# Hybrid diffusion trunk on one core: the last two modulation blocks of a layer computed in the router stage

## The reference

```python
mod = (jax.nn.silu(cond) @ lw['w_ada'] + lw['b_ada'])[:, None, :]
sh1, sc1, gt1, sh2, sc2, gt2 = jnp.split(mod, 6, axis=-1)
h = rmsnorm(x, lw['g_norm1']) * (1.0 + sc1) + sh1
# u = h @ w_in: three branches (differential attention, bidirectional gated
# delta rule, neighbourhood attention) and their gates; merged = gated sum
x = x + gt1 * (merged @ lw['w_out'])
h2 = rmsnorm(x, lw['g_norm2']) * (1.0 + sc2) + sh2
x = x + gt2 * expert_choice_ffn(h2, lw['w_router'], lw['w_e_gate'], lw['w_e_up'], lw['w_e_down'])
```

## Time and profile before

| | |
|---|---|
| median of 3 runs | 3517.86 us (3516.3 to 3520.94) |
| profiled execution | 3521.77 us, its span 3520.0 us |
| mean granted TensorE clock | 0.983 of 2.4 GHz |
| busy: PE, DVE, ACT, POOL | 96%, 37%, 20%, 4% of the span |
| delta stage, layer 0 | about 200 to 789 us of the span |
| router stage, layer 0 | about 1085 to 1193 us of the span |
| chain of waits, by engine | PE 87%, DMA 7%, ACT 3%, DVE 2% |

### The profile page before, as it was taken

The page is one execution under the profiler, slowest core; times in us unless marked ns, Lnnn a source line. Parts: engine busy times, 40 slices in busy tenths (PEclk is TensorE's granted clock), DMA queues, the critical chain, the costliest instruction groups (busy, mean ns, idle before and its releaser), DMA issues.

```text
span 3520.0 us, 47854 instructions
## 1 busy us (share of the span) xinstructions
PE 3388.4 (96%) x20939; PEld 1901.7 (54%) x20939; DVE 1300.3 (37%) x2503; ACT 706.7 (20%) x1536; POOL 157.9 (4%) x179
## 2 busy tenths in 40 slices
PE   7999999999999899999989999999999998999998
PEld 4557767765554544444455577677655554443433
DVE  3354443337542321212243644433464522211213
ACT  3131111115332200000021311111254322000001
POOL 1000000000100000000100000000000000000000
PEclk9999999999999899999999999999999999999998
DMA  7242332341241699999941424232512408999997
GB/s 224 97 125 71 89 100 63 102 115 71 77 171 56 248 383 387 387 395 386 383 141 48 133 63 120 69 107 58 173 48 72 168 31 299 379 396 389 391 389 270
DMA packets 218049, 675.69 MB, mean 192 GB/s; under 512 B 9779, under 2 KB 22297, under 8 KB 214257
## 3 DMA queue, kind: packets, MB, share of 16 engines
q1 hardware_dynamic: 198096, 613.97, 49.6%
q0 software_dynamic: 13312, 43.05, 4.7%
q10 hardware_dynamic: 6432, 15.62, 1.2%
HBM read 605.91 MB, written 66.68 MB: 191 GB/s over the span
## 4 chain that ended last, share of the span: by engine, by line
PE 87%; DMA 7%; ACT 3%; DVE 2%; issue 1%; ACTq 0%; POOL 0%; DVEq 0%; POOLq 0%
PE unit L839 12%; PE unit L787 11%; PE unit L1353 10%; PE work L1356 8%; PE work L1353 6%; PE unit L851 4%; PE unit L830 3%; PE unit L1228 3%; PE unit L870 3%; PE unit L781 3%; DMA arena<-in_w_e_gate 2%; DMA ring<-in_w_e_gate 2%; PE unit L1176 2%; PE work L1041 2%; PE work L1075 2%; PE unit L797 1%
## 5 line engine op out<-in xcount | busy, mean ns | idle before, releaser
L839 PE MATMUL unit<-hT,ring 128*128 128x512 f32 x1024 | 475.5, 593 | 0.0
L1353 PE MATMUL unit<-ring,arena 128*64 128x512 f32 x1568 | 357.1, 601 | 5.3 <-DVE arena L2287 5.3
L2300 DVE SCALAR_TENSOR_TENSOR arena<-work,arena 64x512 f32<-64x512 f32 x64 | 47.9, 749 | 669.4 <-PE work L1353 668.3
L1356 PE MATMUL work<-ring,arena 128*32 128x256 f32 x4608 | 275.4, 382 | 3.9 <-DMA ring<-in_w_e_gate 1.9
L839 PEld LDWEIGHTS unit<-hT,ring 128*128 128x128 f32 x1024 | 177.9, 191 | 140.6 <-issue 140.6
L1353 PEld LDWEIGHTS unit<-ring,arena 128*64 128x64 f32 x1568 | 110.8, 138 | 226.6 <-issue 221.0
L1356 PEld LDWEIGHTS work<-ring,arena 128*32 128x32 f32 x4608 | 136.5, 109 | 164.1 <-issue 79.6
L787 PE MATMUL unit<-hT,ring 128*128 128x512 f32 x512 | 221.1, 592 | 0.0
L1833 ACT ACTIVATE arena<-work 128x512 f32<-128x512 f32 x32 | 19.1, 597 | 846.4 <-PE work L1368 846.4
L1353 PE MATMUL work<-ring,arena 128*64 128x512 f32 x736 | 168.2, 599 | 2.5 <-ACT arena L1834 2.1
L787 PE MATMUL unit<-arena,ring 128*128 128x512 f32 x384 | 166.8, 592 | 0.0
(11 more groups left out here) (448 smaller groups left out, 4737.1 us busy)
## 6 DMA issues: line engine op xcount, KB each, us to landing
ring<-in_w_e_gate SPq DMA_DIRECT2D x50, 2048.0 KB, 14.6
ring<-in_w_e_up SPq DMA_DIRECT2D x48, 2048.0 KB, 14.9
ring<-in_w_e_down SPq DMA_DIRECT2D x46, 2048.0 KB, 16.4
ring<-in_w_in SPq DMA_DIRECT2D x32, 2048.0 KB, 15.4
ring<-in_w_ada SPq DMA_DIRECT2D x24, 2048.0 KB, 8.8
arena<-in_w_e_down SPq DMA_DIRECT2D x18, 2048.0 KB, 15.1
arena<-in_w_e_up SPq DMA_DIRECT2D x16, 2048.0 KB, 14.4
arena<-in_w_e_gate SPq DMA_DIRECT2D x14, 2048.0 KB, 17.5
```

Of the source, the lines that this page charges most:

```text
L839: last = mm(bank[:, :], w[:, k, m * P:(m + 1) * P], hT[:, k, 0:TS], start=k == 0, stop=k == KD - 1)
L1353: last = mm(big[SLS * c:SLS * c + SLS, :], x, w[:, kk, 512 * c:512 * c + 512], start=k == 0, stop=k == KD - 1)
L1356: last = mm(low[SLOTP * c:SLOTP * c + SLOTP, 0:256], xp, w[:, kk, 256 * c:256 * c + 256], start=k == 0, stop=k == KD - 1)
```

## The change

Blocks 10 and 11 leave `FILL` and come last in `PLAN`, behind the output projection's chunks. `EARLY_ADA` is the number of blocks that stay early. TensorE issues block 10 behind the transposes of tiles 4 and 5 and block 11 behind the context tokens' logits, and both folds behind the transposes of the slots. The folds use bank W[3], the copied rows lie in the arena. The bias of `gt2` is added in an instruction of its own behind expert 0's modulated rows. The matrices `gates` and `gatep` are spread behind the first half of expert 0's gate product, in the banks that the down product uses, and the down product of each expert waits for `gates_ready`. On ScalarE the two copies and the two folds come behind `keep_h(8, 10)`, and the copies of the gate matrices behind `keep_x`.

```diff
--- before.py
+++ after.py
@@ -64,9 +64,10 @@
 LATE = [("gc", 0), ("gc", 1)]
 BRANCHES = "bca"
 FILL = []
+EARLY_ADA = 10
 _a = 4
 for _s in [("va", 0), ("qa", 0), ("kc", 0), ("ka", 0), ("qc", 0), ("vc", 0)] + [("g" + b, i) for b in "ab" for i in (0, 1)]:
-    if _a < 12:
+    if _a < EARLY_ADA:
         FILL += [("ada", _a), _s, ("fold", _a)]
         _a += 1
     else:
@@ -75,6 +76,7 @@
 PLAN = [("ada", a) for a in range(4)] + [("qb", 0), ("kb", 0), ("vb", 0), ("zb", 0)]
 PLAN += [_f for _f in FILL if _f[0] != "fold"] + LATE
 PLAN += [("br" + b, i) for b in BRANCHES for i in (0, 1)] + [("wo", 0), ("wo", 1)]
+PLAN += [("ada", a) for a in range(EARLY_ADA, 12)]
 
 
 def kind_of(name):
@@ -398,7 +400,8 @@
         sqsum = rt[:, 1, :]
         xflat = xT.rearrange("p k t -> p (k t)")
         stage = [xflat[:, 512 * i:512 * i + 512] for i in range(NSTAGE)]
-        adarow = [at(7680, (512,)), xflat[:, 512 * NSTAGE:512 * NSTAGE + 512]]
+        adarow = 4 * [at(7680, (512,))] + (EARLY_ADA - 4) * [xflat[:, 512 * NSTAGE:512 * NSTAGE + 512]]
+        adarow += [at(2560 + 512 * i, (512,)) for i in range(12 - EARLY_ADA)]
         (gE, gL, gAT, gD, gDT, gI, gD2, gD2T, gD4, gP, gX, c32, gN, gVB, gKB, gKD) = [
             at(17408 + 512 * i, (H, P)) for i in range(16)]
         gXn, gY, gZT, gV0, gV = gD2, gD2T, gD, gD4, gP
@@ -465,6 +468,9 @@
 
         def tile_t(t):
             return slice(t * P, (t + 1) * P)
+
+        def fold_bank(a):
+            return W[5] if a < EARLY_ADA else W[3]
 
         def last_banks(t):
             return ((W[0], W[1]), (W[3], W[4]), (W[2], W[5]))[t % 3]
@@ -585,7 +591,7 @@
                 sp.dma_start(O["new_diff_v"][0, l].rearrange("t h d -> t (h d)"), aV[:, NTS, :])\
                     .then_inc(sig["new_v_stored"], 16)
                 spilled(*SPILLED[-1])
-                sp.wait_ge(sig["mod_ready"], 12 * (l + 1))
+                sp.wait_ge(sig["mod_ready"], 12 * l + EARLY_ADA)
                 back(flat(K[1]), "kc", 0, "k_loaded")
                 sp.wait_ge(sig["delta_turned"], H * (l + 1))
                 back(flat(Q[1]), "qc", 0, "q_loaded")
@@ -805,7 +811,8 @@
                 if l or a:
                     pe.wait_ge(sig["mod_ready"], 12 * l + a)
                 for m in range(4):
-                    last = mm(W[5][:, 2 * m:2 * m + 2], adarow[a >= 4][:, tile_t(m)], C("fold")[:, 0:2], start=True, stop=True)
+                    last = mm(fold_bank(a)[:, 2 * m:2 * m + 2], adarow[a][:, tile_t(m)], C("fold")[:, 0:2],
+                              start=True, stop=True)
                 last.then_inc(sig["ada_folded"], 1)
                 yield
 
@@ -1211,7 +1218,7 @@
                         project(l, "br" + s, half, dict(a=oaT, b=obT, c=ocT)[s], kk=H)
                         if s == BRANCHES[0] and half == 0:
                             sub_sums()
-                pe.wait_ge(sig["mod2_ready"], l + 1)
+                pe.wait_ge(sig["mod2_ready"], 2 * l + 1)
                 for g in range(2):
                     for k in range(KD):
                         mm(W[0][:, 96 + NE * g:96 + NE * g + NE], mod[:, 24 + k, g:g + 1].to_broadcast([P, P]), wrt[:, k, :],
@@ -1277,6 +1284,8 @@
                 for m in range(4):
                     wo_prompt(1, m)
                 turn_x(4, 6, W[4:6], xT)
+                for _ in ada(l, EARLY_ADA):
+                    pass
                 pe.wait_ge(sig["prompt_added"], 2 * l + 2)
                 router_rows(1, W[3], slice(TS, T), 0)
                 router_rows(1, W[3], slice(TS, T), 4).then_inc(sig["logits_rowed"], 1)
@@ -1286,17 +1295,9 @@
                 last.then_inc(sig["tokens_summed"], 1)
                 pe.wait_ge(sig["logits_copied"], 2 * l + 2)
                 fold_logits((NTS,))
+                for _ in ada(l, EARLY_ADA + 1):
+                    pass
                 turn_x(6, 2 * NT, W[4:6], xT)
-                pe.wait_ge(sig["unit_emptied"], wo_unit(l, 1, None) + 1)
-                for c in range(2):
-                    for k in range(4):
-                        mm(ps[0][SLS * c:SLS * c + SLS, tile_t(k)],
-                           mod[:, 40 + 4 * c + k, 0:1].to_broadcast([P, SLS]), ident, start=True, stop=True)
-                for c in range(4):
-                    for k in range(2):
-                        last = mm(ps[1][SLOTP * c:SLOTP * c + SLOTP, tile_t(k)],
-                                  mod[:, 40 + 2 * c + k, 1:2].to_broadcast([P, SLOTP]), ident, start=True, stop=True)
-                last.then_inc(sig["gates_spread"], 1)
                 pe.wait_ge(sig["aff_ready"], 2 * l + 2)
                 tr(W[1][0:NE, 0:TP], aff[:, NTS, :], ident).then_inc(sig["aff_turned"], 1)
 
@@ -1309,9 +1310,25 @@
                     last = mm(W[5][SLOTP * c:SLOTP * c + SLOTP, 0:NE], best[0:NE, SLS:SLS + SLOTP],
                               ident[0:NE, 0:NE], start=True, stop=True)
                 last.then_inc(sig["slot_turned"], 1)
-                pe.wait_ge(sig["gates_ready"], l + 1)
+                for a in range(EARLY_ADA, 12):
+                    for _ in fold(l, a):
+                        pass
                 turn_x(2 * NT, 3 * NT, (W[4], ps[1]), xT)
                 pe.wait_ge(sig["slots_ready"], 3 * l + 2)
+
+                def spread_gates():
+
+                    pe.wait_ge(sig["slots_ready"], 3 * l + 3)
+                    pe.wait_ge(sig["mod2_ready"], 2 * l + 2)
+                    for c in range(2):
+                        for k in range(4):
+                            mm(W[2][SLS * c:SLS * c + SLS, tile_t(k)],
+                               mod[:, 40 + 4 * c + k, 0:1].to_broadcast([P, SLS]), ident, start=True, stop=True)
+                    for c in range(4):
+                        for k in range(2):
+                            last = mm(W[5][SLOTP * c:SLOTP * c + SLOTP, tile_t(k)],
+                                      mod[:, 40 + 2 * c + k, 1:2].to_broadcast([P, SLOTP]), ident, start=True, stop=True)
+                    last.then_inc(sig["gates_spread"], 1)
 
                 def turn_rows(e):
 
@@ -1337,6 +1354,8 @@
                         else:
                             pe.wait_ge(sig["left_copied"], l * NE + e)
                             pe.wait_ge(sig["right_copied"], l * NE + e)
+                    if kind == "d" and half == 0:
+                        pe.wait_ge(sig["gates_ready"], l + 1)
                     if kind == "d" and half == 0:
                         pe.wait_ge(sig["hidT_ready"], l * NE + e + 1)
                     if kind == "g" and half == 0:
@@ -1372,6 +1391,8 @@
                 for e in range(NE + 1):
                     if e < NE:
                         expert_chunk(e, "g0")
+                    if e == 0:
+                        spread_gates()
                     if e == 0:
                         turn_x(3 * NT, 4 * NT, (W[4], ps[1]), xT)
                         pe.wait_ge(sig["x_kept"], 4 * NT * (l + 1))
@@ -1456,11 +1477,11 @@
             def ada(l, a):
                 n = unit_no(l, "ada", a)
                 big = unit(n)
-                emptied(a_(adarow[a >= 4], big[:, :], ACT.Copy))
+                emptied(a_(adarow[a], big[:, :], ACT.Copy))
 
             def fold(l, a):
                 act.wait_ge(sig["ada_folded"], 12 * l + a + 1)
-                a_(mod[:, 4 * a:4 * a + 4, :], W[5][:, 0:8].rearrange("p (m g) -> p m g", g=2), ACT.Copy)\
+                a_(mod[:, 4 * a:4 * a + 4, :], fold_bank(a)[:, 0:8].rearrange("p (m g) -> p m g", g=2), ACT.Copy)\
                     .then_inc(sig["mod_ready"], 1)
 
             def square(n, k, words=T):
@@ -1751,7 +1772,7 @@
                                     a_(rt1[:, h, 0:TS], W[h][:, :], ACT.Sqrt, bias=eps, scale=1.0 / P)
                                 a_(rt1[:, :, TS:T], h4(W[4]), ACT.Sqrt, bias=eps, scale=1.0 / P)\
                                     .then_inc(sig["sub_rooted"], 1)
-                act.wait_ge(sig["mod2_ready"], l + 1)
+                act.wait_ge(sig["mod2_ready"], 2 * l + 1)
 
                 a_(stat[:, 95:96], eps, ACT.Sqrt)
                 for u in range(KD):
@@ -1815,10 +1836,14 @@
                 keep_h(6, 8)
                 weights_exp(1, prompt)
                 keep_h(8, 10)
+                for a in range(EARLY_ADA, 12):
+                    ada(l, a)
+                for a in range(EARLY_ADA, 12):
+                    fold(l, a)
+                keep_x(2 * NT, 4 * NT)
                 act.wait_ge(sig["gates_spread"], l + 1)
-                a_(gates, ps[0][:, :], ACT.Copy)
-                a_(gatep, ps[1][:, 0:256], ACT.Copy).then_inc(sig["gates_ready"], 1)
-                keep_x(2 * NT, 4 * NT)
+                a_(gates, W[2][:, :], ACT.Copy)
+                a_(gatep, W[5][:, 0:256], ACT.Copy).then_inc(sig["gates_ready"], 1)
 
                 def gate_hidden(e):
 
@@ -2077,9 +2102,9 @@
                 for br in range(2):
                     nb = 2 * l + br
                     if br:
```

(11 more changed lines are left out.)

## The result

The changed kernel took 3529.37 us (median of 6 runs, 3526.31 to 3535.69) beside 3518.89 us (6 runs, 3516.3 to 3526.37) for the kernel before in the same measurement: ratio 1.0029, 95% interval 1.0016 to 1.0043, some 10 us slower. I had forecast 3518 us with 3508 to 3527 for the range; the time is outside, on the slow side. The profiled execution took 3526.7 us, span 3524.9.

What follows compares the result with a forecast made beforehand. TensorE, busy 96% of the span, was taken as the bound. Per layer, 4.5 us won in the delta stage met 4.5 us of router-side cost (2.6 + 1.0 + 0.4 + 0.5): no change, 3518 us, range 3508 to 3527.

Steps and rivals of the forecast that it cites:

- Delta stage, -4.5 us a layer: Delta stage without two blocks: attention starts earlier, -4.5 us a layer, bounds -5.5 (nothing exposed) and -3.
- what could be late next: Attention's start: K and Q, down by about 778, and V were checked and held not late; no size given.
- rival (4): Attention's start: the clock falls at TensorE's new waits, up to 1.5 us a layer, 3521 us; chance 0.1.
- Block 10, 0: Router stage, behind the transposes of tiles 4 and 5: hidden in TensorE's wait for GpSimd, 0, bounds 0 and 2 us.
- Block 11, +2.6: Router stage, ahead of the exponential: fully on the path, 1.94 us at full rate, 3.9 at half, taken as 2.6.
- Last store and gather's issue, +1.0: Router stage: last row store lands beside a load in 7.2 us, gather issued 1.0 us later than by the slots alone.
- The gather, +0.4: Gather of expert 0's rows: the longer measured time beside a load, 7.18 us, taken, costing 0.4 us a layer.
- rival (1): Router stage: loads hold the gather, stores 3 us later, gather 10 us; +5.8 us a layer, 3529 us; chance 0.14.
- Folds, 0: Router stage, ahead of transposes: 1.6 us hidden since TensorE waits for the gather, taken as 0, bounds 0 and 1.6.
- Gate matrices, +0.5: Behind expert 0's first half gate product: delay mostly caught up in a load-bound expert stage, 0.5 us, bounds 0 and 2.3.
- rival (2): Router stage hides nearly everything and denser TensorE work keeps the clock up; -4.7 us a layer, 3508 us; chance 0.12.
- a large effect has no source: Whole kernel: 5.5 us of TensorE work per layer is moved and none removed, so no change was expected.

Runs made afterwards that it cites:

- e3: Changed kernel with ScalarE's squares and root of the last group ahead of its copy of the last gap's filler; 3526.95 us, 1.0010 of the kernel before.
- e8: Changed kernel with gate matrices ahead of expert 0, squares before filler copy, two loads held, two transposes ahead of block 11; 3504.30 us, 0.9959 of before.
- e5: Kernel before, with the load of expert 0's fourth half held until the gathered rows have landed; 3515.19 us, 0.9984 of the kernel before.
- e4: Changed kernel with the loads of expert 0's two up halves held until its rows have landed; 3526.68 us, 1.0012 of the kernel before.
- e9: e8 with block 10 folded in TensorE's wait for VectorE's maxima; 3501.28 us, 0.9942 of the kernel before.
- e1: Changed kernel with the gate matrices spread ahead of expert 0's first product; 3524.12 us, 1.0007 of the kernel before.
- e2: Changed kernel with six filler places taken off the delta stage's start, so the list ends as before; 3533.39 us, 1.0029 of the kernel before.
- e7: Changed kernel with only block 11 moved, to block 10's place, and block 10 back in the delta stage; 3527.82 us, 1.0019 of the kernel before.
- e10: e8 without the hold on expert 0's third and fourth half loads; 3514.93 us, 0.9983 of the kernel before.
- e11: e8 with block 11 again ahead of the transposes of steps 6 and 7; 3512.25 us, 0.9977 of the kernel before.
- e12: e8 with ScalarE's copy of the last gap's filler again ahead of the squares; 3512.64 us, 0.9977 of the kernel before.

## Why the prediction was wrong

The terms were the right ones and are separate, as the experiments show: each can be taken away by itself. The sum was wrong because one gain was lost by half and three costs were under-sized. Over both layers the delta stage gave 4.8 us less than forecast, the gather cost 3.3 us more, the gate matrices 4.0 and block 11 1.4; the last store and the issue cost 0.7 less. By the prediction's steps:

- **Delta stage, -4.5 us a layer: measured -2.1 / -2.1.** The head turns do run closer, and attention did not wait for K, Q or V. The step that failed is the question what could be late next: K, Q and V were the whole list. What I left out is that a shift of six places also moves the end of each filler product against ScalarE's fixed order of copies. One now ends in the last tick of the gap ahead of the squares, so its copy, which ScalarE issues first, goes at 772.08, and the squares wait. It was a copy that was late. e3 gives 1.5 us back, and e8, where the clock stays up as well, reaches -5.3 / -5.2: the bound of -5.5 was near the truth for a kernel without that copy.
- **Clock at the new waits.** I named it as a rival (4), for attention's start at 1.5 us a layer, and held it within no change. It fell elsewhere: behind the wait ahead of the first head turn, which the copy had made longer (5.30 us for 3.60, 1.7 us a layer). At attention's start, where I looked for it, it was 1.00 (784 to 800).
- **Block 10, 0: right.** 1.90 us in the wait for GpSimd, 3.58 us to the column sums as before.
- **Block 11, +2.6: measured +3.1 / +3.5.** The clock fell within the block (1.00 from 1168 to 1169, 0.76 in the next microsecond, then 0.50); the mechanism and the order on ScalarE were right.
- **Last store and gather's issue, +1.0: measured +0.6 / +0.7.** The store lands in 6.6 / 6.7 us, where 7.2 was taken.
- **The gather, +0.4: measured +2.5 / +1.6.** This is the second step that failed, on rival (1)'s ground. I took 7.18 us as the price "beside a load". By e5 a gather alone needs 4.1 us, and 6.23 was a gather with a load beside it for 5.4 of its 6.2 us (issued at 1180.15, 8.4 us to landing). In the changed kernel the load issued at 1184.15 lands after 12.5 us, at 1196.6, and is there from the gather's first microsecond to its last. The Trainium skill (DMA: Bandwidth & Descriptors, Queues, rings and completion order) says that a DMA engine takes turns between the queues that have work. An estimate from that rule and e5's figure: with two busy queues throughout, 4.1 us become 8.2. The runs agree roughly: 8.69 and 8.76 were measured, 8.1 to 10.0 in all kernels without the hold that have a moved block. For the kernel before, with the load there for 5.4 us, the same estimate gives 6.8, where 6.2 was measured. The rule that I used against the slower case for the store was the one that gave the gather's price.
- **Folds, 0: right only because the gather was late.** With the loads held they are the bound (e4), and 2.3 / 2.6 us of the stage (e8 to e9).
- **Gate matrices, +0.5: measured +2.6 / +2.4 in expert 0, and not caught up.** This is the third step that failed. I took the expert stage as bound by its weight loads, from one row of 18.02 us on the chain. But TensorE is busy for 495.7 of the 500 us from 1246 to 1746 in the kernel before, and waits for loads for 2.0 us there and 2.8 in layer 1, in the changed kernel for 1.3 and 1.9: that is all there was to give back. The window and the two waits of the kernel before, layer 0 (window as above; waits in us in total, times, longest):

```profile
1246.00:1746.00 500.00, 495.69 (x4438) 200.27 (x4434) 97.77 (x206) 25.28 (x58) 44.69 (x48) 1.00 1.03 388
...
PE work L1356 <- DMA arena<-in_w_e_gate: 1.4, 2, 0.9
PE work L1356 <- DMA ring<-in_w_e_gate: 0.6, 1, 0.6
```

The other experts took 0.3 us more in layer 0; the 2.4 us less in layer 1 are within what that stretch varies by. Of the cost, 2.1 us are the matrices and the rest is expert 0's first product at half clock a little longer (6.54 us for 6.05). That their place can also bring this product to 3.65 us, as in e1, I had not seen: rival (2) had that gain, but from denser work in general.

The sum that I made was 4.5 - 4.5 = 0; that measured in the stages is 9.1 - 2.1 in layer 0 and 5.5 - 2.1 in layer 1. The reasoning that "a large effect has no source", since TensorE's work is only moved, was the wrong guide: the moved work stays the same, and waits and half clock are what it is exchanged for. Rival (1) was right in sign, and in half of its mechanism: the loads slow the gather. But its 3 us of a late store did not come, the gather needed 8.7 us and not 10, and it left the delta stage and the gate matrices as forecast. That its number, 3529 us, is the one measured is luck.

What stays open: which of the two clock levels a wait leads to. With a wait of 4.1 us ahead of the first head turn the fillers behind it ran slow (5.1 to 5.6 us for eight) in all 10 layers recorded. With 2.57 us they took 3.60 us in 11 of 18 layers and 4.5 to 5.3 us in the other 7, four of them all those of e2 and e7. So in these runs the clock always fell behind the longer wait, and behind the shorter one in some layers and not in others.

## What to carry to other kernels

Work moved off a saturated engine's chain paid here only once its neighbours were put in order: look at which in-order copy now ends in the last tick ahead of a wait, not only at the loads. A duration read from a trace is a duration with its company; before it is reused for a more crowded place, work out what shared the queue with it and what it costs alone. And a load with slack can be worth holding back while a small transfer on the chain is in flight: holding one load in the unchanged kernel gained 5.9 us, more than half of what the change lost.

## What the runs showed of the hardware

- Loads of 2 MB held until the gather had landed took 11.0 to 21.3 us to land and cost expert 0 nothing (49.0 / 49.1 us in e8 with the hold, 49.2 / 49.0 in e10 without it).
- The last store of the rows, 512 KB on ScalarE's queue, landed after 3.9 / 3.7 us in the kernel before and 2.6 / 3.4 in e5, with no load in flight, and after 6.6 / 6.7 us in the changed kernel, beside a load and with the DMA share at 1.0.
- The gather of expert 0's rows landed after 3.9 to 4.3 us where the loads were held (e4, e5, e9, e11, e12; in e8 the held load went 4.9 / 4.2 us after the gather's issue), after 6.2 / 7.2 in the kernel before and 8.7 / 8.8 in the changed one.
- 32 small matmuls in a wait of VectorE's (2.47 + 0.66 us, mean clock 0.68) left TensorE at 2.4 GHz for the product behind: 3.65 us for 16 instructions that took 6.05 to 6.54 us behind an idle wait.
